# Router products among the last dense groups, narrow projections in column groups, fewer routing steps

## What is computed

```python
# first block: dt_raw is 8 of the columns of h @ w_in
z, xbc, dt_raw, q, k, v = jnp.split(h @ w_in[l], IN_SPLITS, axis=-1)
# second block: gm is 16 of the columns of h @ w_in_2 (the mLSTM gates)
qa, ka, va, qm, km, vm, om, gm, mg = split_cols(proj, IN_SPLITS_2)
x = x + u @ w_out[l]
x = x + hier_moe(rmsnorm_2(x, norm2_g[l]), ...)
# hier_moe
g_logits = xf @ w_rg + b_rg                     # 4 groups
g_idx = jnp.argmax(g_logits, axis=-1)
e_logits = xf @ w_re + b_re                     # 32 experts, those of the best group count
top_v, top_i = lax.top_k(e_in, 2)
top_w = jax.nn.softmax(top_v, axis=-1) * p_group[:, None]
# each token row goes to its two experts: (silu(x w_gate) * (x w_up)) w_down, weighted and added
```

## Time and profile before

| | |
|---|---|
| three runs | 2050.21 us median, 2049.18 to 2054.14 |
| the profiled execution | 2049.78 us, of which the span of the profile is 2048.0 |
| TensorE (PE) matmuls busy | 1787.7 us, 87% of the span |
| VectorE (DVE), ScalarE (ACT), GpSimd (POOL) busy | 544.4, 326.0, 43.9 us |
| chain that ended last | PE 71%, DMA 19%, DVE 5%, ACT 3% |
| HBM | 327.89 MB read, 35.15 MB written |

### The profile page before, as it was taken

How to read it: one execution, slowest core, us unless ns; L and a number is a source line. 1 busy time by engine, 2 the same in 40 slices (tenths; PEclk the granted TensorE clock), 3 DMA queues, 4 the chain that set the end, 5 groups by cost and what they waited for, 6 DMA issues and landing times.

```text
span 2048.0 us, 15632 instructions
## 1 busy us (share of the span) xinstructions
PE 1787.7 (87%) x5930; PEld 817.7 (40%) x5930; DVE 544.4 (27%) x1207; ACT 326.0 (16%) x664; POOL 43.9 (2%) x70
## 2 busy tenths in 40 slices
PE   6999999989999999989899788999748787877872
PEld 2455544434444444436344444444522222222221
DVE  4312445432222200122765233311320000000002
ACT  2111223221111100001233323210100000000000
POOL 0004000000000000000000000000010000000001
PEclk9999989999999999999999899999769999999996
DMA  9667520012211121221111100123249999999995
GB/s 395 226 246 246 185 82 1 32 66 82 82 50 73 62 85 69 97 87 72 41 42 41 41 22 20 65 100 123 83 175 428 428 428 429 427 429 428 429 427 193
DMA packets 37891, 360.33 MB, mean 176 GB/s; under 512 B 4088, under 2 KB 6536, under 8 KB 18512
## 3 DMA queue, kind: packets, MB, share of 16 engines
q1 hardware_dynamic: 23216, 310.56, 37.4%
q0 software_dynamic: 7008, 25.43, 3.6%
q10 hardware_dynamic: 7616, 23.66, 3.0%
HBM read 327.89 MB, written 35.15 MB: 177 GB/s over the span
## 4 chain that ended last, share of the span: by engine, by line
PE 71%; DMA 19%; DVE 5%; ACT 3%; issue 1%; POOL 1%; SPq 0%; ACTq 0%; DVEq 0%
DMA upper<-in_w_expert_down 16%; PE bank L875 15%; PE bank L533 11%; PE bank L551 8%; PE bank L1177 6%; PE bank L997 5%; PE bank L966 3%; PE bank L1005 3%; PE bank L695 2%; PE bank L596 2%; PE bank L619 2%; PE bank L837 2%; PE bank L956 2%; PE bank L685 1%; PE bank L855 1%; PE bank L606 1%
## 5 line engine op out<-in xcount | busy, mean ns | idle before, releaser
L1177 PE MATMUL bank<-slot,arena 128*64 128x512 f32 x1024 | 370.8, 661 | 102.0 <-DMA slot<-in_w_expert_gate 52.9
L875 PE MATMUL bank<-hT,slot 128*128 128x512 f32 x704 | 304.6, 596 | 6.6 <-ACT hT L1898 6.6
L1177 PEld LDWEIGHTS bank<-slot,arena 128*64 128x64 f32 x1024 | 110.9, 152 | 341.3 <-issue 239.3
L1177 PE MATMUL bank<-upper,arena 128*64 128x512 f32 x512 | 228.2, 599 | 0.0
L875 PEld LDWEIGHTS bank<-hT,slot 128*128 128x128 f32 x704 | 134.5, 191 | 176.7 <-issue 175.6
L533 PE MATMUL bank<-arena,slot 128*128 128x512 f32 x352 | 153.0, 598 | 3.3 <-DVE arena L1572 3.3
L1863 DVE TENSOR_TENSOR arena<-arena,bank 128x512 f32<-128x512 f32 x16 | 11.0, 687 | 458.9 <-PE bank L1177 458.9
L551 PE MATMUL bank<-hT,slot 128*128 128x512 f32 x272 | 125.7, 621 | 7.7 <-DVE hT L1602 6.5
L997 PE MATMUL bank<-hT,slot 128*128 128x512 f32 x256 | 121.4, 623 | 12.0 <-ACT arena L1898 10.4
L533 PEld LDWEIGHTS bank<-arena,slot 128*128 128x128 f32 x352 | 67.4, 192 | 88.9 <-issue 84.8
L1561 DVE SCALAR_TENSOR_TENSOR arena<-bank,cols,arena 128x511 f32<-128x511 f32 x44 | 33.0, 749 | 213.4 <-ACT arena L2073 213.4
(11 more groups left out here) (333 smaller groups left out, 1749.3 us busy)
## 6 DMA issues: line engine op xcount, KB each, us to landing
slot<-in_w_expert_gate SPq DMA_DIRECT2D x32, 2048.0 KB, 17.5
upper<-in_w_expert_down SPq DMA_DIRECT2D x16, 2048.0 KB, 24.2
slot<-in_w_expert_down SPq DMA_DIRECT2D x16, 2048.0 KB, 19.7
slot<-in_w_expert_up SPq DMA_DIRECT2D x16, 2048.0 KB, 19.5
upper<-in_w_expert_up SPq DMA_DIRECT2D x16, 2048.0 KB, 24.2
slot<-in_w_in SPq DMA_DIRECT2D x15, 2048.0 KB, 7.7
slot<-in_w_ada SPq DMA_DIRECT2D x12, 2048.0 KB, 14.6
slot<-in_w_up SPq DMA_DIRECT2D x11, 2048.0 KB, 7.7
```

What stands on the lines that cost most here:

```text
L875: ins = pe.matmul(bank[4 * j + c][:, :], w[:, k, half:half + P], hT[:, k, :], start=(k == 0), stop=(k == KD - 1))
L1177: ins = pe.matmul(dst[b * CAP:(b + 1) * CAP, :], lhs(b, k), rhs(b, k), start=(k == 0), stop=(k == n_k - 1))
```

## The change

1. The dt and gate weights are padded to 32 columns and become the stationary operand: `narrow` is 8 matmuls of 512 columns in four column groups, whose partial sums lie on four groups of 32 partitions. VectorE copies the bank to SBUF (`dtw`, `gmw`), and `folded` adds the four groups and turns the result to token rows by four small products with `fold`. For dt the fold stands after the second matmul of the first Z group, for the gates after the second QM group. `w_gm` is loaded by ACT before the feed-forward part and not at the start. VectorE adds the gate bias right ahead of the first variance of the head norms.
2. The logits of features 0 to 5 are formed as three pairs of 512-column products between the `G_WO2` groups, feature 6 and 7 behind the last group as small products. ACT writes the scaled copies and the squares of `xT` after each group, VectorE adds the squares, and four products with a column of ones sum them. The logits are summed, multiplied by the norm and biased in steps for all tokens at once.
3. ACT evicts the transposed halves, once plain to `xtok` and once scaled to `htok`, after its first exponential.
4. Ranks and counts are two products with 128 columns each. Constants are made earlier, and the number of blocks is found by one comparison with a table `g7` and one reduction.

```diff
+            def narrow(w, bk):
+
+                for k in range(KD):
+                    g = slice(32 * (k % 4), 32 * (k % 4) + 32)
+                    ins = pe.matmul(bank[bk][g, :], w[:, k, :], hT[:, k, :], start=(k < 4), stop=(k >= 4))
+                return ins
+
+            def folded(wide, bk, n):
+
+                for t in range(NT):
+                    ins = pe.matmul(bank[bk][:, t * n:(t + 1) * n], wide[:, t * P:(t + 1) * P], fold[:, 0:n], start=True, stop=True)
+                return ins
...
-                pe.wait_ge(S["ld_small"], 48)
-                for t in range(NT):
-                    ins = full_k(0, lambda k: hT[:, k, t * P:(t + 1) * P], lambda k: w_dt[:, k, :],
-                                 sl=bank[6][:, t * 8:t * 8 + 8])
-                ins.then_inc(S["dt_full"], 1)
+                pe.wait_ge(S["ld_small"], 32)
+                narrow(w_dt, 6).then_inc(S["wide_full"], 1)
                 come("z")
-                token(G_Z, slot(0, KD, 512), 0)
+                wz = slot(0, KD, 512)
+                free(G_Z)
+                for k in range(KD):
+                    if k == 2:
+                        pe.wait_ge(S["wide_row"], 1)
+                        folded(dtw, 6, 8).then_inc(S["fold_full"], 1)
+                    ins = pe.matmul(bank[home[G_Z]][:, :], hT[:, k, 0:P], wz[:, k, :], start=(k == 0), stop=(k == KD - 1))
...
-                for t in range(NT):
-                    ins = full_k(0, lambda k: hT[:, k, t * P:(t + 1) * P], lambda k: w_gm[:, k, :],
-                                 sl=bank[5][:, t * 16:t * 16 + 16])
-                ins.then_inc(S["gt_full"], 1)
+                pe.wait_ge(S["ld_gm"], 16)
+                narrow(w_gm, 5).then_inc(S["wide_full"], 1)
...
                 feature(G_QM + 1, slot(2, KD, 512), P)
+                pe.wait_ge(S["wide_row"], 2)
+                folded(gmw, 5, 16).then_inc(S["fold_full"], 1)
...
+                def logits(k):
+
+                    pe.wait_ge(S["xg_rdy"], k + 2)
+                    for b in range(2):
+                        ins = pe.matmul(bank[4][64 * b:64 * b + 36, :], w_rt[:, k + b, :], hT[:, k + b, :],
+                                        start=(k == 0), stop=(k == 4))
+                    if k == 4:
+                        ins.then_inc(S["lg_full"], 1)
+
+                def logits_of(k, at):
+
+                    pe.wait_ge(S["xg_rdy"], k + 1)
+                    for t in range(NT):
+                        ins = pe.matmul(bank[5][:, at + t * 36:at + (t + 1) * 36], hT[:, k, t * P:(t + 1) * P], w_rt[:, k, :],
+                                        start=True, stop=True)
+                    ins.then_inc(S["lg_full"], 1)
+
+                for m in range(KD):
+                    i, c = m // 4, m % 4
+                    if c == 0:
+                        come(f"wo2_{i}")
+                    feature(G_WO2 + m, slot((2, 1)[i], KD, 512), c * P, uT)
+                    if m in (2, 4, 6):
+                        logits(m - 2)
+                pe.wait_ge(S["lw_ev"], 2)
+                for t in range(NT):
+                    for b in range(2):
+                        r = slice(64 * b, 64 * b + 36)
+                        ins = pe.matmul(bank[6 + b][:, t * 36:(t + 1) * 36], lgw[r, t * P:(t + 1) * P], ident[r, r],
+                                        start=True, stop=True)
+                ins.then_inc(S["lg_full"], 1)
+                logits_of(6, 0)
             if on("route"):
+                pe.wait_ge(S["sq_sum"], 4)
+                for t in range(NT):
+                    ins = pe.matmul(bank[7][:, 256 + t:257 + t], sqr[:, 0, t * P:(t + 1) * P], ones[:, 0:1], start=True, stop=True)
+                ins.then_inc(S["ss_full"], 1)
+                logits_of(7, 144)
...
+                oh = R["ohs"].rearrange("p t e -> p (t e)")
+                pe.matmul(bank[3][:, 0:NT * E], tris[:, :], oh, start=True, stop=True)
+                pe.matmul(bank[3][:, NT * E:2 * NT * E], ones[:, :], oh, start=True, stop=True).then_inc(S["rank_full"], 1)
...
+                ve.wait_ge(S["wide_full"], 1)
+                tell(ve.tensor_copy(dtw, bank[6][:, :]), "wide_row")
+                ve.wait_ge(S["fold_full"], 1)
...
+                    if 2 <= m < KD - 1:
+                        squares_added(sqr, m - 1, 3 * KD + m, False)
+                    if m == KD - 2:
+                        squares_added(sqr, m, 3 * KD + m + 1, False)
+                        ve.wait_ge(S["lg_full"], 1)
+                        tell(ve.tensor_copy(lgw[64:100, :], bank[4][64:100, :]), "lw_ev")
...
+                ve.wait_ge(S["lg_full"], 2)
+                seq(ve.tensor_copy(R["la"], bank[6][:, 0:NT * 36].rearrange("p (t e) -> p t e", e=36)))
+                seq(ve.tensor_tensor(R["la"], R["la"], bank[7][:, 0:NT * 36].rearrange("p (t e) -> p t e", e=36), ALU.add))
+                ve.wait_ge(S["lg_full"], 3)
+                seq(ve.tensor_tensor(R["la"], R["la"], bank[5][:, 0:NT * 36].rearrange("p (t e) -> p t e", e=36), ALU.add))
+                squares_added(sqr, KD - 1, 4 * KD, True)
+                ve.wait_ge(S["ss_full"], 1)
+                tell(ve.tensor_scalar(rsq, bank[7][:, 256:256 + NT], 1.0 / D, EPS, ALU.mult, ALU.add), "row_var")
...
+                seq(ve.tensor_copy(fs[:, 1, :], tot_[:, 0, :]))
+                for t in (1, 2):
+                    seq(ve.tensor_tensor(fs[:, t + 1, :], fs[:, t, :], tot_[:, t, :], ALU.add))
+                seq(ve.tensor_tensor(R["ct"], fs[:, 3, :], tot_[:, 3, :], ALU.add))
+                seq(ve.tensor_tensor(R["rk"], fs, bank[3][:, 0:NT * E].rearrange("p (t e) -> p t e", e=E), ALU.add))
+                seq(ve.tensor_tensor(R["cm"], blast(R["ct"], 7), bmid(R["g7"], E), ALU.is_gt))
+                seq(ve.tensor_reduce(R["nb"], R["cm"], AX, ALU.add))
+                seq(ve.tensor_scalar(R["be"][:, 0, :], R["nb"], 0.0, None, ALU.mult))
                 seq(ve.tensor_tensor_scan(R["cin"], R["nb"], R["be"][:, 0, :], 0.0, ALU.add, ALU.add))
...
-            for dst, name in ((w_dt, "w_dt"), (w_gm, "w_gm_2"), (w_rt, "w_router")):
+            for dst, name in ((w_dt, "w_dt"), (w_rt[:, :, :], "w_router")):
...
+                ac.wait_ge(*emptied(G_WA))
+                ac.dma_start(w_gm.rearrange("p k n -> p (k n)"), a["w_gm_2"]).then_inc(S["ld_gm"], 16)
...
+                for m in range(KD):
+                    ac.wait_ge(*emptied(G_WO2 + m))
+                    if m < KD - 1:
+                        act(hT[:, m, :], xT[:, m, :], ACT.Copy, "xg_rdy", scale=col("norm2", m))
+                    act(sqr[:, m, :], xT[:, m, :], ACT.Square, "sq_part")
...
+                for x in range(2 * NT):
+                    t, half = x // 2, slice((x % 2) * 512, (x % 2 + 1) * 512)
+                    ac.wait_ge(S["xk_full"], x + 1)
+                    if x == 0:
+                        ac.wait_ge(S["lg_rdy"], 1)
+                        act(R["ge"], R["gs"], ACT.Exp, "lg_exp")
+                    act(xtok[:, t, half], bank[x % 2][:, :], ACT.Copy)
+                    act(htok[:, t, half], bank[x % 2][:, :], ACT.Copy, "xk_ev", scale=rsq[:, t:t + 1])
                 ac.wait_ge(S["top_rdy"], 1)
                 act(R["ed"], R["d"], ACT.Exp, "lg_exp")
```

More of the change, by code:

```diff
@@ L117, in two_blocks @@
         block1 = sb("block1", [P, P])
-        w_dt = sb("w_dt", [P, KD, 8])
-        w_gm = sb("w_gm", [P, KD, 16])
+        fold = sb("fold", [P, 32])
         w_rt = sb("w_rt", [P, KD, 36])
@@ L177, in two_blocks @@
         y2 = view(arena, 15384, 512)
+        w_dt = view(arena, 8216, KD, 32)
+        dtw = view(arena, 9240, 512)
+        w_gm = view(arena, 15360, KD, 32)
+        gmw = view(upper, 6656, 512)
         acsT = arena[0:HEADS, 16384:16384 + T]
@@ L1140, in _ @@
                 pe.wait_ge(S["u_rdy"], KD)
-                for i in range(2):
-                    come(f"wo2_{i}")
-                    for c in range(4):
-                        feature(G_WO2 + 4 * i + c, slot((2, 1)[i], KD, 512), c * P, uT)
-            if on("route"):
+                def logits(k):
[26 more added lines that the diff above has]
+                logits_of(6, 0)
+            if on("route"):
+                pe.wait_ge(S["sq_sum"], 4)
[3 more added lines that the diff above has]
+                logits_of(7, 144)
                 pe.wait_ge(*emptied(G_WO2 + 7))
@@ L1604, in _ @@
                 empties(G_QA, G_QM - G_QA)
[L1605 to L1607 removed]
+                ve.wait_ge(S["wide_full"], 2)
+                tell(ve.tensor_copy(gmw, bank[5][:, :]), "wide_row")
                 ve.wait_ge(S["pads"], 1)
@@ L1623, in _ @@
                 own("dve_free")
+                ve.wait_ge(S["fold_full"], 2)
+                tell(ve.tensor_tensor(gt, bank[5][:, 0:64].rearrange("p (t e) -> p t e", e=16), bmid(row("gate_b"), NT), ALU.add),
+                     "gt_rdy")
                 q_variance(0)
@@ L1775, in _ @@
                 ve.wait_ge(S["row_root"], NT + MH + 1)
                 seq(ve.reciprocal(rsq, rsq))
```

(11 more changed lines are left out.)

93 lines of the change are left out of this document (36 added, 57 removed).

## The result

| | kernel before | changed kernel |
|---|---|---|
| time, median of 4 runs | 2052.18 us (2049.18 to 2057.76) | 2018.89 us (2018.01 to 2021.05) |
| ratio, with its 95% interval | | 0.9832 (0.9809 to 0.9856) |
| span of the profiled execution | 2048.0 us | 2016.5 us |

The changed kernel is 1.7% faster. Between the medians lie 33.3 us, between the two profiled executions 31.5 of span. Forecast were 2015.0 us and a gain of 35.2, counted from the 2050.21 of the first three runs of the kernel before; from there the gain is 31.3. The executions of the kernel before spread over 8 us, those of the changed kernel over 3.

The account below looks back on a forecast made before the run. The expert stage is bound by DMA, but cuts ahead of the first pair move it whole. Gains of 8.0 (dt), 9.5 (gates) and 17.7 (router) sum to 35.2: 2050.2 - 35.2 = 2015.0 us, range 2012 to 2023.

Parts of the forecast that it names:

- What bounds: Expert stage: bound by DMA, turns stay 31.85 us; whatever is cut ahead of the first expert pair moves the whole stage.
- Part 1: dt projection: narrow products, fold and Z group take 9.54 us instead of 17.53, a gain of 8.0.
- Part 2: Gate projection: products, fold and two groups behind take 16.4 us instead of 25.9, a gain of 9.5.
- Part 3: Router, last group to slots plus added pairs: 26.5 us against 44.25, a gain of 17.7.
- rival (a): Router: the clock falls at once behind the dense groups and stays low; +3.8 us, 2018.8; chance 0.13.
- The copy's cover: dt projection: VectorE's copy of the wide row ends 1.0 us before TensorE asks for it, so Z doesn't stall.
- worst case: Router with a low clock and a visible table load: 31.6 us, a gain of only 12.6.
- VectorE's new idle time: Router, behind the one-hots: VectorE waits some 4.4 us for the second exponential, queued behind ACT's evictions.
- Rival (b): Router: evictions and transposes run in turn, 18.2 us instead of 9.4, time 2023.8; chance 0.05.
- Rival (c): Both projections and router pairs: column groups don't overlap, 12.7 us back, 2027.7; chance 0.11 including its milder form.
- milder form: One projection: something fixed in time takes the slack, giving up 8.0 or 9.5 us, 2023 to 2024.5.
- Rival (d): Expert weight stream: turns 2.3 us longer each make the kernel slower; chance 0.03 with anything else not faster.

Follow-up runs that it names:

- the array kept busy: Changed kernel plus two unused 512-column products in TensorE's gap ahead of the router's sums of squares: 2018.44 us.
- ranks between the halves: Changed kernel with the second exponential moved behind the sixth eviction and the rank products behind the fourth half's transposes: 2012.32 us.
- pairs together: Changed kernel with the three pairs of router products one behind the other after the seventh output group: 2018.36 us.
- the gap filled: Changed kernel plus two unused 512-column products in TensorE's gap ahead of the first attention: 2016.22 us; with three router repairs too, 2009.85 us.

## Why the prediction was right

The time, 2018.89, is inside the range and 3.9 us over the forecast. What bounds the kernel and parts 1 and 2 came out as reasoned; part 3 was 2.9 us too hopeful, and a term that the sum lacks, 3.4 us lost in the first attention, was mostly covered by small gains elsewhere that the sum lacks too. That the end came as close as 3.9 us is in part luck. So is the meeting with the 2018.8 of rival (a), whose mechanism gave 1.4 of its 3.8 us. Step by step:

- **What bounds.** Right. 31.8 us gained at the first pair are 31.5 at the end; the turns didn't change, and the two differences behind them, 1.7 us lost in the last product and 1.9 gained in the last load, nearly cancel.
- **Part 1.** 8.0 forecast, 7.97 read in the next shared landmark (144.29 against 152.26): right. The copy's cover was 1.2 us, forecast 1.0: copied by 113.97 + 0.69 = 114.66, fold at 115.82, no gap in Z. That undoing it costs 8.0 in time is no second proof: in that profile the attention starts 10.1 us later (270.09), the first pair 7.8, since the attention is shorter again with the old products. Another 1.0 us came by 260 us in this profile, within the scatter of that landmark, and then the term that the sum lacks took 3.4 back (below).
- **Part 2.** 9.5 forecast. From the start of the QA groups to that of the squares behind the second QM group are 942.23 - 882.16 = 60.1 us, before 957.90 - 888.31 = 69.6: 9.5 read, right. Undone it is 10.4 to 11.4 in time; in the undone kernel's profile the same stretch is 953.51 - 884.14 = 69.4, so 9.3 again, and 2.0 of its lateness were there at 884.14, ahead of the gates.
- **Part 3.** 17.7 forecast, 14.8 read. Three terms were too small: the pairs 3.55 instead of 2.6; lg_rdy 8.4 instead of 8.0; and lg_rdy to the slots 17.4 instead of 15.9, of which 1.28 is the table load for the exponential and the rest the evictions at 1.16 a half, just over the 1.15 named as a sign of being wrong. The forecast's worst case had the table load; the sum had not. I had put both table loads under VectorE's steps. That held for the root's, whose load ran at 1440.49 while VectorE summed. It failed for the exponential's: the load stands in ScalarE's program behind the wait for lg_rdy, so it starts when its operand is there, with ScalarE idle for 2.91 us ahead of it. In the kernel before, the same exponential had a single wait in front of it, and its load ran at 1462.31, 15 us ahead of the exponential (1477.28); now two waits stand there, for the transposes and for lg_rdy. With the array kept busy the transposes of the first half were done over 1 us ahead of lg_rdy (1447.83) and the load still came at 1447.91. Whether the second wait alone makes the difference no run shows. The kernel that loaded the table early got 1.3 us in the stretch.
- **VectorE's new idle time.** Forecast as 4.4, measured as 6.04, by the mechanism foreseen: the second exponential stands behind sixteen evictions. The ranks between the halves show that it was worth 5.7 us together with the place of the rank products.
- **Rival (a)**, the clock falling at once: in part. It fell 3.6 us behind the last group, right behind the gap of 1.44 us ahead of the sums, and not at once; filling the gap gave 1.4 us in the stretch, all of it ahead of lg_rdy. The clock's price there was 1.4 of the 3.8 that this rival would have cost.
- **Rival (b)** fell: (1457.70 - 1448.43)/8 = 1.16 us a half, not 2.3. Evictions of one half lie over the transposes of the other, with 0.25 us open a pair of halves. **Rival (c)** fell by the kernel with one column group; of its milder form, slack taken by something else in one projection, the attention's 3.4 us are a cousin, though no transfer was the cause. **Rival (d)** fell with the turns.
- **The term that was not in the sum.** Ahead of the feed-forward part the first attention took 151.24 us from 260.03 on, against 147.83 from 269.01 on before. The same stretch (from there to the start of the feed-forward part) is 147.9 in the other two profiles with the old dt products, 151.2 in seven of the eight with the new ones in four column groups and the gap unfilled, 148.3 in the eighth (pairs together, the same program up to there) and in that with one column group (148.2), and 146.0 in both with the gap filled. It goes with how long the low clock lasts, 7, 14 or 20 us, and the kernel that shortens the low clock shortens the stretch. That the clock costs this much is shown. That the dt change makes it last longer is not: one profile with the same program had the short one, and no run here separates the products from the time at which they end. The feed-forward part and the second block gave another 0.6 and 1.1 us, also unforecast; their cause is open. The sum read from the profiles is 8.0 + 1.0 - 3.4 + 9.5 + 1.7 + 14.8 = 31.6, against 31.8 at the first pair. Of the 3.6 us under the forecast's 35.2, part 3 has 2.9 and the terms outside the three parts 0.7: the attention's 3.4 less 2.7 of gains that nobody forecast.

## What to carry to other kernels

A narrow projection in the middle of dense work costs twice, by its instructions and by the clock of the groups behind it: make the narrow side the stationary operand, put it in column groups, and fold afterwards; both parts paid as their rows said. When evictions move to the engine that also owes a small result, place that result by when its consumer wants it and not behind the bulk: moving it, and the rank products with it, was worth 5.7 us of the stretch and 7.6 in time, of which some 2 arose in the expert stage. Look at the clock behind a gap of a microsecond or two ahead of small products: filler products there gave 1.4 us in one stretch and 4.6 in the other, 3.1 of them at the last scatter, but neither gain is clear of the scatter of the times. And where kernels with the same program up to a landmark reach it up to 2.9 us apart, as here the attention, read a part's worth between two near landmarks and not from the end.

## What the runs showed of the hardware

- Eight fp32 products of 512 columns took 6.85 us in one column group, 1.72 in four, with 32 columns of weights each.
- The clock falls while TensorE counts as busy: with 8 or 16 moving columns in dense work it was 0.80 and 0.77 on the mean, though TensorE was busy for the whole stretch; with 512 columns and 32 columns of weights it was 1.00. In the kernel with the gates as before it was 1.00 up to 932, 0.50 from 934 to 942, and so low in the first dense group behind too (the narrow products end at 936.9).
- Transposes of 128x128 didn't bring the clock down in the kernel before: it was still 1.00 at 1461, when the last of them had ended at 1458.1. The Trainium skill (TensorE: Matmul & The Clock Gate, Part 4: PE-mode transpose) says that they don't count as activity for the clock. This trace didn't show a fall from them, and no run here tells what the clock stood on.
- A table load ran ahead of its function's operand with one wait in front of it (at 1462.31 for an exponential at 1477.28, kernel before), and behind it with two (at 1447.02, changed kernel).
- Filling a gap moved the fall and shortened the low stretch, but 1.5 of the 4.6 us gained in the attention were gone again by the last scatter, 0.9 of them in the feed-forward part. Why is open.
